# Seven block products for eight in the projection back of the feed-forward

## The reference

```
first:   f = (silu(x @ w_gate[l]) * (x @ w_up[l])) @ w_down[l]
         x = layernorm(ALPHA * x + f)
second:  x = x + 0.5 * swiglu(rms_norm(x), w_gate, w_up, w_down)
swiglu(h, w_gate, w_up, w_down) = (silu(h @ w_gate) * (h @ w_up)) @ w_down
```

## Time and profile before

| | us |
|---|---|
| runs, median of 3 | 3848.74 (3847.14 to 3856.86) |
| profiled execution, span | 3849.1 (the page gives no other time of it) |
| TensorE busy | 3699.7 (96%) |
| VectorE, ScalarE, GpSimd busy | 1356.9, 1427.8, 1321.5 (35%, 37%, 34%) |
| one entry of 1024 columns: ScalarE, GpSimd, mean | 1.054, 2.405 |

### The profile page before, as it was taken

How to read it: one execution, slowest core, us unless ns; L and a number is a source line. 1 busy time by engine, 2 the same in 40 slices (tenths; PEclk the granted TensorE clock), 3 DMA queues, 4 the chain that set the end, 5 groups by cost and what they waited for, 6 DMA issues and landing times.

```text
span 3849.1 us, 54988 instructions
## 1 busy us (share of the span) xinstructions
PE 3699.7 (96%) x23392; PEld 3068.2 (80%) x23392; DVE 1356.9 (35%) x2865; ACT 1427.8 (37%) x2476; POOL 1321.5 (34%) x630
## 2 busy tenths in 40 slices
PE   9998999999899999999998899999999999889999
PEld 8877888878688888888767788888888866778887
DVE  2455111344611132112676631112111486752111
ACT  3454222335432233223555432224222456534222
POOL 3113444421154434444321034444444321114443
PEclk9999999999999999999999999999999999999999
DMA  4102333311133323333210023433333220013332
...
DMA packets 406645, 291.90 MB, mean 76 GB/s; under 512 B 18016, under 2 KB 356864, under 8 KB 406400
## 3 DMA queue, kind: packets, MB, share of 16 engines
...
q0 software_dynamic: 288, 1.18, 0.1%
...
## 4 chain that ended last, share of the span: by engine, by line
PE 85%; DVE 8%; ACT 5%; issue 1%; POOL 1%; DMA 0%; SPq 0%; DVEq 0%; ACTq 0%; POOLq 0%
PE ps L762 13%; PE ps L763 13%; PE ps L761 13%; PE ps L887 7%; PE ps L890 7%; PE ps L889 7%; PE ps L1505 3%; PE ps L981 2%; PE ps L999 2%; PE ps L990 1%; PE ps L788 1%; PE ps L1061 1%; PE ps L790 1%; PE ps L789 1%; POOL wl L3208 1%
## 5 line engine op out<-in xcount | busy, mean ns | idle before, releaser
L3208 POOL TENSOR_TENSOR wl<-wraw,wh 128x1024 fp32r<-128x1024 f32 (+2 forms) x532 | 1247.0, 2345 | 2233.2 <-ACT wh L2569 2233.0
L2569 ACT ACTIVATE wh<-wraw 128x1024 fp32r<-128x1024 f32 (+2 forms) x532 | 548.0, 1032 | 1072.0 <-PE ps L890 558.4
L761 PE MATMUL ps<-x_T,wh 128*128 128x512 f32 (+1 forms) x2224 | 850.2, 382 | 0.0
L763 PE MATMUL ps<-x_T,wl 128*128 128x512 f32 (+1 forms) x2224 | 848.9, 382 | 0.0
L762 PE MATMUL ps<-x_T,wh 128*128 128x512 f32 (+1 forms) x2224 | 848.9, 382 | 0.0
L761 PEld LDWEIGHTS ps<-x_T,wh 128*128 128x128 f32 x2224 | 418.3, 188 | 80.7 <-issue 0.5
L762 PEld LDWEIGHTS ps<-x_T,wh 128*128 128x128 f32 x2224 | 418.3, 188 | 80.4 <-issue 0.5
L763 PEld LDWEIGHTS ps<-x_T,wl 128*128 128x128 f32 x2224 | 418.2, 188 | 80.1
L887 PE MATMUL ps<-wh,h_T 128*128 128x512 f32 x1120 | 437.5, 391 | 4.7 <-DVE x_tm L2522 2.8
L890 PE MATMUL ps<-wh,h_T 128*128 128x512 f32 x1120 | 436.2, 389 | 0.0
L889 PE MATMUL ps<-wl,h_T 128*128 128x512 f32 x1120 | 436.1, 389 | 0.0
...
## 6 DMA issues: line engine op xcount, KB each, us to landing
...
```

Of the source, the lines that this page charges most:

```text
L761: mm(b[:, t0:t1], wh[:, k, :], xTh[:, k, t0:t1], k == 0, False)
L763: ins = mm(b[:, t0:t1], wl[:, k, :], xTh[:, k, t0:t1], False, k == 7)
L2569: copy(hl_of(w)[0], raw_of(w)).then_inc(*s.sig("w", "hi", w))
L3208: tt(wl, raw_of(w), wh.bitcast(F32), ALU.subtract).then_inc(*g.sig("w", "lo", w))
```

## The change

The 22 blocks are taken in four groups of 6, 6, 4 and 6. In the first three groups the blocks are taken in pairs. A pair is a product of matrices of 2 x 2 blocks: the activation's are two row halves by two hidden blocks, the weights' two hidden blocks by two column halves. It is made with seven block products in Winograd's form. Which sums of activation blocks are needed is in `hF` (seven forms per pair, `forms` on VectorE and high halves on ScalarE); the weights' sums are T1 to T4 (`sums_in`, `sum_T3`, `sum_T4`, VectorE). w_down is no longer loaded through the list for these groups but whole, 256 rows by 1024 a pair, with one DMA of 1 MB into `down` (`down_in`, SyncE). A product has a number from 1 to 7; (7, 1) is product 7 of pair 1. `FAST` gives the order, `units` in an entry being two products of 512 columns, each with its own high half (ScalarE) and low half (GpSimd, or VectorE for those in `FAST_DVE`). A product sums over the pairs in one PSUM bank for each of two row tiles `a`; products 1 and 2, 7 and 4, 5 and 3 share banks, and `down_sums` on VectorE combines and adds them to x_tm. The group of the last six blocks is done as before, in halves of three entries, with `late=3` in the second half.

The diff at its core, with less indentation; counts in the programs of GpSimd and SyncE follow the longer list (`N_FFN` entries where 68 stood).

```diff
+GROUPS = (6, 6, 4, 6)
+FAST = {3: [((1, 0), (1, 1)), ((6, 0), (6, 1)), ((1, 2), (6, 2)), ((7, 0), (7, 1)), ((7, 2), (5, 0)), ((5, 1), (5, 2)),
+            ((2, 0), (2, 1)), ((2, 2), (4, 0)), ((4, 1), (4, 2)), ((3, 0), (3, 1)), ((3, 2),)],
+        2: [((1, 0), (6, 0)), ((1, 1), (6, 1)), ((7, 0), (5, 0)), ((7, 1), (5, 1)), ((2, 0), (2, 1)), ((4, 0), (4, 1)),
+            ((3, 0), (3, 1))]}
+FAST_DVE = ((5, 1), (5, 2), (4, 1), (4, 2))
+FORM = {1: 2, 2: 0, 3: 6, 4: 1, 5: 3, 6: 5, 7: 4}
+ENDS = 2 * (GROUPS[3] // 2)
+N_FFN = 2 * NF + sum(len(FAST[n // 2]) for n in GROUPS[:3]) + ENDS
...
 def ffn(g, u, d, l):
-    for grp in range(2):
-        for i in range(11):
-            f(g, l, (11 * grp + i) * P, P)
-            f(u, l, (11 * grp + i) * P, P)
-        for half in range(2):
-            t(d, l, 11 * grp * P, 11, half * 512, 512)
+    f0 = 0
+    for grp, size in enumerate(GROUPS):
+        for i in range(f0, f0 + size):
+            f(g, l, i * P, P)
+            f(u, l, i * P, P)
+        if grp < 3:
+            n = l if d == "w_down" else l + 2
+            for e, units in enumerate(FAST[size // 2]):
+                out.append(((d, l, f0 * P, len(units), ("fast", grp, e), 512), (n, grp, units)))
+        else:
+            for half in range(2):
+                t(d, l, f0 * P, size, half * 512, 512)
+        f0 += size
...
+hF = h_T[:, 0:10752].rearrange("p (q c m t) -> p q c m t", q=3, c=2, m=7)
+hB = scr_all[:, 0:2048].rearrange("p (b t) -> p b t", b=8)
+down = [cut(10752, 2048), mix[:, 0:2048], mix[:, 2048:4096]]
+sums = [cut(12800, 512), scr[6], scr[7]]
+def fast_src(prod, q):
+    if prod in (6, 4):
+        return sums[q]
+    o = {1: 0, 7: 0, 5: 512, 2: 1024, 3: 1536}[prod]
+    return down[q][:, o:o + 512]
+def fast_ready(n, g, prod, q):
+    return (f"down{q}", n, g) if prod < 4 else ("fast", {4: "T4", 5: "T1", 6: "T2", 7: "T3"}[prod], n, g, q)
...
+def fast(n, g):
+    bks = {}
+    for prods in ((6,), (1, 2), (7, 4), (5, 3)):
+        for a in range(2):
+            bks[prods[0], a] = bank(("fast", n, g, prods[0], a), ("fast", {6: "y", 1: "x11", 7: "x21", 5: "x12"}[prods[0]], n, g, a))
+            bks[prods[-1], a] = bks[prods[0], a]
+    pairs = GROUPS[g] // 2
+    for units in FAST[pairs]:
+        w = use()
+        wh, wl = hl_of(w)
+        for u, (prod, q) in enumerate(units):
+            first, m = prod in (6, 1, 7, 5), FORM[prod]
+            pe.wait_ge(*at("ffn", "form", n, g, q, m > 2))
+            pe.wait_ge(*at("w", "lo", w, u))
+            for a in range(2):
+                b, free = bks[prod, a]
+                t = slice(a * P, (a + 1) * P)
+                if q == 0:
+                    pe.wait_ge(*(free if first else at("fast", {2: "u2", 4: "v", 3: "z"}[prod], n, g, a)))
+                mm(b[:, :], hF[:, q, 0, m, t], wh[:, u, :], first and q == 0, False)
+                mm(b[:, :], hF[:, q, 0, m, t], wl[:, u, :], False, False)
+                ins = mm(b[:, :], hF[:, q, 1, m, t], wh[:, u, :], False, q == pairs - 1)
+                if q == pairs - 1:
+                    ins.then_inc(*pe.sig("fast", prod, n, g, a))
+                elif a and u == len(units) - 1:
+                    ins.then_inc(*pe.sig("w", "used", w))
+        pe.also("w", "used", w)
...
+def fast_low(n, g, prod, q):
+    w, u = unit_of[n, g, prod, q]
+    wh, wl = hl_of(w)
+    v.wait_ge(*at("w", "hi", w, u))
+    tt(wl[:, u, :], fast_src(prod, q), wh[:, u, :].bitcast(F32), ALU.subtract).then_inc(*v.sig("w", "lo", w, u))
+def sums_in(n, g, q):
+    v.wait_ge(*at(f"down{q}", n, g))
+    if g:
+        v.wait_ge(*at("w", "lo", *unit_of.get((n, g - 1, 4, q), (0, 0))))
+    b11, b12, b22 = fast_src(1, q), fast_src(5, q), fast_src(3, q)
+    step(tt(b12, b11, b12, ALU.subtract), "fast", "T1", n, g, q)
+    tt(sums[q], b22, b12, ALU.add).then_inc(*v.sig("fast", "T2", n, g, q))
+def sum_T3(n, g, q):
+    v.wait_ge(*at("w", "lo", *unit_of[n, g, 1, q]))
+    tt(fast_src(7, q), sums[q], fast_src(1, q), ALU.subtract).then_inc(*v.sig("fast", "T3", n, g, q))
+def sum_T4(n, g, q):
+    v.wait_ge(*at("w", "lo", *unit_of[n, g, 6, q]))
+    v.wait_ge(*v.own())
+    tt(sums[q], sums[q], fast_src(2, q), ALU.subtract).then_inc(*v.sig("fast", "T4", n, g, q))
+def forms(n, g, q):
+    v.wait_ge(*v.own())
+    step(tt(hB[:, 4:6, :], bc(hB[:, 3:4, :], [P, 2, 256]), hB[:, 1:3, :], ALU.add))
+    step(tt(hB[:, 6, :], hB[:, 4, :], hB[:, 2, :], ALU.add))
+    tt(hB[:, 7, :], hB[:, 6, :], hB[:, 0, :], ALU.add).then_inc(*v.sig("ffn", "sums", n, g, q))
+    for part, (b0, m0, k) in enumerate(((0, 0, 3), (4, 3, 4))):
+        v.wait_ge(*at("ffn", "hi", n, g, q, part))
+        tt(hF[:, q, 1, m0:m0 + k, :], hB[:, b0:b0 + k, :], hF[:, q, 0, m0:m0 + k, :].bitcast(F32),
+           ALU.subtract).then_inc(*v.sig("ffn", "form", n, g, q, part > 0))
+def down_sums(n, g, finish, base):
+    Y, X, V, Z = ([psum_of("fast", n, g, prod, a) for a in range(2)] for prod in (6, 1, 7, 5))
+    def add(j, half, b, key, first=False, minus=False):
+        hs = slice(512 * half, 512 * half + 512)
+        if first and base and not g:
+            v.wait_ge(*at(*base(j, half)))
+        v.wait_ge(*v.own())
+        finish(xtm[:, j, hs], first and not g, b, minus).then_inc(*v.sig("fast", key, n, g, j % 2))
+    for a in range(2):
+        v.wait_ge(*at("fast", 1, n, g, a))
+        v.wait_ge(*at("fast", "copy", n, g, a))
+        tt(Y[a][:, :], X[a][:, :], scr[4 + a], ALU.subtract).then_inc(*v.sig("fast", "u2", n, g, a))
+    for prod, q in FAST_DVE[:2]:
+        if q < GROUPS[g] // 2:
+            fast_low(n, g, prod, q)
+    for a in range(2):
+        add(a, 1, Y[a], "y", True)
+        add(2 + a, 0, Y[a], "y", True, True)
+        add(2 + a, 1, Y[a], "y", True, True)
+    for a in range(2):
+        v.wait_ge(*at("fast", 7, n, g, a))
+        add(2 + a, 1, V[a], "v", minus=True)
+    for a in range(2):
+        v.wait_ge(*at("fast", 5, n, g, a))
+        add(2 + a, 1, Z[a], "z", minus=True)
+    for prod, q in FAST_DVE[2:]:
+        if q < GROUPS[g] // 2:
+            fast_low(n, g, prod, q)
+    for a in range(2):
+        v.wait_ge(*at("fast", 2, n, g, a))
+        add(a, 0, X[a], "x11", True)
+    for a in range(2):
+        v.wait_ge(*at("fast", 4, n, g, a))
+        add(2 + a, 0, V[a], "x21", minus=True)
+    for a in range(2):
+        v.wait_ge(*at("fast", 3, n, g, a))
+        add(a, 1, Z[a], "x12")
...
+    for g, size in enumerate(GROUPS[:3]):
+        pairs = size // 2
+        for f in range(size):
+            sg = scr[4 + f % 2]
             wg = use()
             wu = use()
...
+            v.wait_ge(*at("ffn", "sig", n, g, f))
+            step(tt(sg, sg, psum_of("F", wg)[:, :], ALU.mult), "ev", wg)
+            if f == size - 1:
+                for q in range(pairs - 1):
+                    sum_T3(n, g, q)
             v.wait_ge(*at("w", "used", wu))
...
+            h = hB[:, 0:2, :] if f % 2 else hB[:, 2:4, :]
+            tt(h, sg.rearrange("p (b t) -> p b t", b=2), psum_of("F", wu)[:, :].rearrange("p (b t) -> p b t", b=2),
+               ALU.mult).then_inc(*v.sig("ev", wu))
+            v.also("ffn", "h", n, g, f)
+            if f % 2:
+                forms(n, g, f // 2)
+            if size - pairs - 1 <= f < size - 1:
+                sums_in(n, g, f - (size - pairs - 1))
+        use(len(FAST[pairs]))
+        sum_T3(n, g, pairs - 1)
+        for q in range(pairs):
+            sum_T4(n, g, q)
+        down_sums(n, g, finish, base)
...
-s.wait_ge(*at(f"w{w % NRAW}", w))
+M = weights[w][1]
 if w >= NHL:
     s.wait_ge(*at("w", "used", w - NHL))
+if isinstance(M, tuple):
+    n, g, units = M
+    for u, (prod, q) in enumerate(units):
+        s.wait_ge(*at(*fast_ready(n, g, prod, q)))
+        copy(hl_of(w)[0][:, u, :], fast_src(prod, q)).then_inc(*s.sig("w", "hi", w, u))
+    continue
...
+for g, size in enumerate(GROUPS[:3]):
+    for f in range(size):
+        if g == 1 and f == 0:
             aside()
...
+        sg = scr[4 + f % 2]
         wg = use()
...
+        use()
         s.wait_ge(*at("w", "used", wg))
...
+        if f > 1:
+            s.wait_ge(*at("ffn", "h", n, g, f - 2))
+        elif g:
+            s.wait_ge(*at("fast", "u2", n, g - 1, f))
+        act(sg, psum_of("F", wg)[:, :], ACT.Sigmoid).then_inc(*s.sig("ffn", "sig", n, g, f))
+        if f == size - 1:
+            use()
+        if f % 2:
+            q = f // 2
+            s.wait_ge(*at("ffn", "h", n, g, f))
+            copy(hF[:, q, 0, 0:3, :], hB[:, 0:3, :]).then_inc(*s.sig("ffn", "hi", n, g, q, 0))
+            s.wait_ge(*at("ffn", "sums", n, g, q))
+            copy(hF[:, q, 0, 3:7, :], hB[:, 4:8, :]).then_inc(*s.sig("ffn", "hi", n, g, q, 1))
+    use(size // 2 - 1)
+    for a in range(2):
+        s.wait_ge(*at("fast", 6, n, g, a))
+        copy(scr[4 + a], psum_of("fast", n, g, 6, a)[:, :]).then_inc(*s.sig("fast", "copy", n, g, a))
+    use(len(FAST[size // 2]) - size // 2)
...
+M = weights[w][1]
+if isinstance(M, tuple):
```

(34 more changed lines are left out.)

137 lines of the change are left out of this document (72 added, 65 removed).

## The result

| | before | after |
|---|---|---|
| runs, median of 4 | 3847.94 us (3846.67 to 3856.86) | 3907.28 us (3899.61 to 3909.73) |
| profiled execution, span | 3849.1 us | 3897.8 us |

The ratio is 1.0141, 95% interval 1.0124 to 1.0157: the kernel became slower, by 54 us by this ratio. The two medians lie 59 us apart and the two profiled executions 48.7 us. The profiled execution of the change is the fastest of its four: the others took 7 to 10 us more, at a mean granted clock of 0.976 to 0.978 where it has 0.979. The forecast was 3895 us, slower.

A forecast was written before the change was run, and what follows sets the result against it. TensorE, busy 96% of the span, was taken as the bound. Fewer matmuls, -65.3 us, and stalls, (10.9 + 6.3 + 1.25) x 6 = +110.7, gave +45: 3895 us, range 3862 to 3912 (chance 0.56).

The forecast's parts named there:

- One round of 1.69: VectorE and GpSimd alternating on 512-wide SBUF pieces: VectorE ends 0.54 us after GpSimd, GpSimd 1.15 after VectorE.
- rival B: Fast groups: slower clock after stalls comes on top, nothing absorbed, 18 x 1.7 us, 3925 us; chance 0.09.
- What was costed at nothing: w_down loads, earlier pairs' sums, PSUM banks, norm behind the last half: 0 us; 1 to 3 a group if cover fails.
- A: Fast groups: VectorE and GpSimd overlap without blocking, stalls 4.75 x 6 = 28.5 us, 3812 us; chance 0.20 including up to 3837.
- D: Whole kernel a wash: stalls of 10.9 us per feed-forward cancel the saving, 3837 to 3860 us; chance 0.11.
- C: Whole kernel: full saving, VectorE always meets an idle GpSimd and all is early, 3784 us; chance 0.04.
- (1): Sign in the matmul count: 23392 - 288 = 23104 matmuls.
- (2): Sign: TensorE gaps before (5,1) and (4,1) released by VectorE, and before (1,1) of the two-pair group.
- (3): Sign on VectorE: low halves of weights and T4 at means of 1.2 to 1.7 us.
- (5): Sign: one wait for GpSimd of 1.25 us near each feed-forward's end.
- (4): Sign on GpSimd: its 512-wide pieces at about 1.5 us.
- (6): Sign: slices at the lower clock inside feed-forwards.

The follow-up runs named there:

- run 3: The change with GpSimd's low halves of the products' weights written 8 columns wide instead of 512, output not the reference's: 3824.25 us, ratio 0.9928.
- run 5: The change with `late=2`: two pieces instead of three taken tile by tile in the plain group's last half: 3900.66 us, ratio 1.0138.
- run 10: run 7 without run 6's product order; against the change only VectorE's queue is reordered: 3842.0 us, ratio 0.997.
- run 7: The change with VectorE's queue ordered by TensorE's need (Y additions last), together with run 6's edits: 3824.41 us, ratio 0.9942.
- run 6: The change with two-pair groups reordered: (7,0), (5,0) before (1,1), (6,1); T3 earlier; low half (5,1) on GpSimd: 3890.96 us, ratio 1.0107.
- Run 2: The change with the six Y additions of `down_sums` moved behind the low halves (4,x): 3854.75 us, ratio 1.0004.
- run 8: run 7 with `late=2`, two pieces taken tile by tile at the plain group's end: 3830.31 us, ratio 0.9954.
- run 9: run 7's queue with `late=2` and groups of 6, 6, 6 and a plain one of 4: 3834.55 us, ratio 0.9953.

## Why the prediction came out as it did

*The mechanism and the sign* were right. VectorE and GpSimd shut each other out when both have all operands in SBUF; run 3 takes this away and the three-pair groups lose nothing. The sum of the change, by its own terms:

| | predicted | measured | over the kernel, measured |
|---|---|---|---|
| 288 matmuls fewer | -65.3 | -65.3 (23104 left) | -65.3 |
| three-pair group | +5.45 | +4.33 | x 12 = +52.0 |
| two-pair group | +6.3 | +9.2 | x 6 = +55.0 |
| plain group | +1.25 | +1.16 | x 6 = +7.0 |
| sum | +45 | | +48.7 |

The last column's sum is the 48.7 us between the two spans. That it meets them to a tenth is partly chance: over the six feed-forwards, each from its first gate matmul of 512 columns to the same matmul behind its norm, the change adds 7.4 to 8.5 us, 47.0 together, and 1.7 us lie outside. With the same program ahead of it, the first feed-forward starts at 357.4 us in this execution and at 354.6 in run 5's, so a few microseconds of a span are not the change's. The range 3862 to 3912 us holds the 3907.28 of the runs, 12 above the forecast. Three terms were mis-sized, and two of the errors nearly cancel: -1.12 x 12 = -13.4 and +2.9 x 6 = +17.4 us. That the sum came within 4 us of the profiled difference is luck to that extent.

*The three-pair group, 1.1 too much.* Up to the differences the chain holds to 0.2 us: the low halves of the forms end at 5.5 and 7.0 after the start (predicted 5.69 and 7.03), T4 at 13.8 (13.79), the differences at 15.0 (15.23). Then I let the low half (5,1) find GpSimd busy as in every round, to 16.72. In the trace VectorE's two PSUM differences had left GpSimd free to go on; its instruction ended at 429.98, and VectorE's low half, issued at 429.94, took its turn at once. One round of 1.69 became one of 0.68 (0.67 or 0.68 in all twelve groups). (5,2) ended at 17.3 instead of 18.41, and everything behind it stands 1.1 earlier: (4,2) at 27.3 instead of 28.40, the end at 32.9 instead of 34.0. The round was right, the place in the alternation wasn't: the two instructions with a PSUM operand come between, and GpSimd's turn passes beside them.

*The two-pair group, 2.9 too little.* The mis-sized term is the clock, which was put at nothing. The waits themselves came as predicted: 2.82 before (1,1) for 3.1, 0.40 before (4,0) for 0.9, 2.48 before (4,1) for 2.2, together 5.7 for 6.2. Behind the first and the third the granted clock was 0.51 and 0.50 for 3.4 us, each with 8 matmuls at 0.43 us from start to start for 0.227, 1.6 to 1.7 us lost. I took both at 0, "as both stalls come ahead of the binding one". That is wrong for the second: the wait before (4,1) is the last of its group, and no later wait of VectorE is there to take its slow matmuls in. From (4,1) to the next product the group takes 5.8 us where 18 matmuls are 4.1; the 1.7 us count in full. For the first, the premise "VectorE's queue, which doesn't slow" failed. Run 10 shows it: with the same wait VectorE's low half (4,1) ends 0.9 to 1.2 us later where the clock fell. In the change, GpSimd's 1024-wide piece ahead of that low half ends 21.7 us after the start (20.6 by the prediction's figures), its high half having waited 1.56 us for TensorE to free the buffer, and the low half (5,1) met a piece of GpSimd (1.73 us for 0.75). TensorE starts (4,1) 22.3 us after the start instead of 21.3. 1.1 and 1.7 make the 2.8; how the 1.1 divides between the clock, the low half (5,1) and additions at a pitch of 0.75 for 0.72, no run separates. So rival B was nearly true for one group in three, and 0 for the other two, whose waits of 0.86 and 1.33 us leave the clock at 1.00. The range 0 to +31 us held it (the two drops are 3.3 x 6 = 20 us of slow matmuls, of which 2.8 x 6 = 17 reach the end).

*The plain group* is in order: one wait for GpSimd of 1.05 us (0.89 of it shown as idle) and the slower matmul behind it, by the buffer that comes free too late. *What was costed at nothing* held: the gate and up stretches between the groups lose nothing in all but two places (0.1 and 0.6 us).

*Rivals.* A fell, since the engines exclude each other, but its figures for the kernel without blocking were good ones: run 3 shows 0 and, in three of the six two-pair groups, 4.1 for its 0 and 3.5. D asked for stalls of 10.9 us per feed-forward; they are 19.0, and 9.2 of them are the two-pair group's. C is refuted by the measured time, and run 3 shows stalls that need no blocking.

*What would show it.* (1), (2) and (3) came as written, (5) with 1.05 us for 1.25. Of (3) the means are 1.32 to 1.67, of (4) 1.47 to 1.57. (6) came in the two-pair groups, not in all.

Two things the prediction had not asked. How much hangs on the order of VectorE's queue: with VectorE and GpSimd blocking each other as before (T4 still takes 1.59 us in the mean in run 7), the queue alone brings the loss in the fast groups from 107 to 43 us (run 10), and together with run 6's edits to 30.5 (run 7). And that delays in one queue are not simply moved: run 1 moved T4 behind the low halves (5,x), and the kernel lost 33 us, for VectorE then stood idle ahead of them and the next in the queue (V) had a bank to release. Run 2's single edit brought 52. What stays open is the 1.6 us that a three-pair group still loses in run 7: waits of 0.6 and 0.2 us before (4,1) and (4,2), the rest in delays of 0.1; no run separated them. The mixed answer of runs 5, 8 and 9 at the norm was seen in the waits, not tested further.
